# Where FoX's projection steps stand in a body of sixteen units: four together behind the first transposes, against two there and two ahead of the value products

## The chip, the cores and the metric

The kernel runs on one NeuronCore of a Trainium2 chip. The metric is the device time of one execution in microseconds (us). TensorE (PE) multiplies, and loads its stationary operand in a second instruction (PEld); VectorE (DVE), ScalarE (ACT) and GpSimd (POOL) work beside it, and SyncE (SP) issues DMAs. Each engine takes its own instructions in the order in which they are written and stops at a semaphore wait, with all that stands behind it.

## The reference

One layer of a hybrid decoder trunk over 1024 tokens of width 1024, in float32:

```
h = rms_norm(x); p = h @ w_in
x += concat[FoX attention | Mamba-2 SSD | GLA | HGRN2] @ w_out
x += cross_attention(rms_norm(x), rms_norm(mem))
x += conv_glu(rms_norm(x))
```

The change lies in FoX, the forgetting attention. It has 4 heads of width 64, and for each block of 128 queries it computes

```
logits = q @ k.T * scale + cum_log_f[query] - cum_log_f[key]   # keys up to the block's end
probs  = softmax(where(causal, logits, -1e30))
o      = probs @ v, then rms_norm over each head
```

## The kernel before

**Stages.** The mixers are computed one after another: HGRN2, FoX, SSD, GLA; then the output projection, cross attention and the feed-forward part. The one combined projection `h @ w_in` is not a stage of its own. It is cut into column groups of 128 ("items"), each item into two halves of 512 tokens, each half into 8 steps. A step (`fill`, line 1278) is three matmuls of 128x512, which take the float32 product as high times high, low times high and high times low part (lines 100 to 102). Steps of the next mixer are spread between the instructions of the present one, so that PE has work while ACT and DVE do softmax and evictions. Tables say how many steps stand at each place: `spread` (line 144) turns a list of counts into ranges of steps, and `_FX` (line 169) is the list for FoX. The first six counts are for FoX's preparation (`FOX_PRE`), the others come in pairs, one pair for each of the 16 units of the body: `FOX_A[u]` and `FOX_B[u]`.

**The body of FoX.** A unit u is a pair of heads and a block of 128 queries, i = u mod 8; its keys are i+1 blocks of 128. In this text the pieces of PE's work in a unit are called as follows:

- T0, T1 (line 1460): transposes of the probabilities of the two heads, key blocks 0 to 3 and, where i is 4 or more, 4 to 7. Each head's transposes wait for that head's exponential (`expd`), and for the eviction of the group two before in the same PSUM bank (`p_ev`).
- A and B: the steps `FOX_A[u]` and `FOX_B[u]`, two each before.
- S0, S1 (line 1450): the scores of unit u+2, keys 0 to 511 and, where they exist, the rest. A score piece goes to one of three banks in turn and waits until DVE has read the piece three before (`sc_read`).
- X (line 1441): small extra products, in units 1, 2, 3, 4, 9, 10, 11 (two) and 13.
- O (lines 1470 and 1476): the row sums' inverses spread over a bank, and the products of the probabilities with the values.

Their order on PE is T0, A, T1, S0, X, B, S1, O; in unit 0 A stands ahead of T0.

**The other engines in a unit.** ACT takes, in this order: the evictions of T0 and T1 (line 709), the eviction of X (line 692 or 687; for a norm lines 574 and 576), in every other unit the eviction of a projection half (`copy_out`, line 518), the exponentials of unit u+1 for both heads (line 699, each with an accumulator read that completes it), and in every fourth unit the high part of the next weights (line 505). DVE takes the inverse of the sums (1058), the normalisation of unit u-1 (1063, 1065), the logits of unit u+2 from the score banks (1039 and 1045), their maxima (1054), and at times the low part of the weights (852).

The choice of halves that ACT and DVE handle in a unit goes by the first step of `FOX_A[u]` and the last of `FOX_B[u]` (`begun`, line 161).

Of the kernel before, what the change touches and what calls it, by code (L numbers as in the profile page):

```python
# [21 lines left out]
KT = D // P  # L22
# [111 lines left out]
H0, F0, S0, G0 = 1, 9, 15, 21  # L134
# [9 lines left out]
def spread(first, last, counts):  # L144

    out, m = [], first
    for c in counts:
        out.append((m, m + c))
        m += c
    assert m == last  # L150
    return out
# [4 lines left out]
def in_two(spans):  # L156

    return spans[0::2], spans[1::2]
# [6 lines left out]

_HG = spread(2 * F0 * KT, 2 * S0 * KT, [16] * 4 + [2, 2] * NT)
HG_PREP, (HG_A, HG_B) = _HG[:4], in_two(_HG[4:])
_FX = spread(2 * S0 * KT, 2 * G0 * KT, [6, 6, 5, 5, 5, 5] + [2, 2] * 16)
FOX_PRE, (FOX_A, FOX_B) = _FX[:6], in_two(_FX[6:])
_SD = spread(2 * G0 * KT, 2 * N_ITEMS * KT, [12] * 4 + [5, 5] * 4 + [4, 4] + [0, 0] * 3)  # L170
SSD_CONV, (SSD_A, SSD_B) = _SD[:4], in_two(_SD[4:])
# [2333 lines left out]
```

How the kernel before makes its waits and increments, by code:

```python
            def link(ins):  # L257
                count[0] += 1
                ins.then_inc(E(s), 1)
                eng.wait_ge(E(s), count[0])
# [67 lines left out]
        @block.sync  # L328
        def _(sp):
            w = a["w_in"][0]
            narrow = ((0, OFF_FF, 4), (DT_ROW, OFF_DT, 4), (GA_ROW, OFF_GA, 16))
            def x_tile(i):
                sp.dma_start(MX[:, i, :], x[i * P:(i + 1) * P, :]).then_inc(x_loaded[i], 16)
            sp.dma_start(LNX, a["ln_mix"][0].partition_broadcast(P)).then_inc(E("ln_loaded"), 16)
            for i in range(3):
                x_tile(i)
            sp.wait_ge(E("zeroed"), 1)
            with nc.allow_non_contiguous_dma(reason="narrow column groups and parameter columns"):
                for row, off, n in narrow:
                    sp.dma_start(WR[:, 0, :, row:row + n], w[:, off:off + n].rearrange("(k p) c -> p k c", p=P))\
# [19 lines left out]
                                a["ssd_d"][0, h:h + 1].rearrange("(p o) -> p o", o=1).to_broadcast([64, 1])))  # L361
                for dst, src in par:
                    sp.dma_start(dst, src).then_inc(E("params"), 16)
                assert len(par) == N_PAR
            for n in range(RAW, N_ITEMS):
                sp.wait_ge(E("g_lo"), n - RAW + 1)
                if n == G0 + 3:
                    sp.wait_ge(E("av_ev"), len(PAIRS))
# [11 lines left out]
            for j in range(KV_ITEMS):  # L380
                if j == KV_ITEMS // 2:
                    sp.wait_ge(E("gl_e1"), 1)
                    sp.wait_ge(E("gl_e2"), 1)
```

## Time and profile before

| | |
|---|---|
| median of 3 runs | 1709.78 us (1709.38 to 1710.87) |
| the profiled execution | 1708.04 us, of which its span 1706.3 us |
| PE busy | 1641.3 us, 96% of the span |
| DVE, ACT, POOL busy | 794.6, 662.8, 74.3 us |
| TensorE's granted clock, mean | 0.989 |

The span runs from the first to the last instruction that the profile shows; 1.7 us of the execution lie around it. PE is the engine that is nearly always busy, and the chain of work that ended last runs over it. The FoX body lies from 294.5 us, where unit 0's A starts, to 408.7 us, where unit 15's O ends.

### The profile page before, as it was taken

To read this page: it belongs to the slowest core of one execution; us is meant where nothing else is said; L and a number is where in the kernel's file an instruction comes from. 1 tells how busy PE (TensorE), PEld (TensorE's weight loads), DVE (VectorE), ACT (ScalarE), POOL (GpSimd) and SP (SyncE) were. 2 spreads that over 40 slices of the span, in tenths; PEclk is the share of its full clock that TensorE was granted. 3 is DMA by queue.
4 is the path that set the end of the run, shared out by engine and by line. 5 is a ranking of instruction groups with operands and counts; after the bars stand their busy time and mean duration, and the time that the engine had idled before them with its cause. 6 is when DMAs were issued, how large, how long until landed. Compare 5 with 4: busy or idle time off the path is not lost.

```text
span 1706.3 us, 20672 instructions
## 1 busy us (share of the span) xinstructions
PE 1641.3 (96%) x8070; PEld 1318.6 (77%) x8070; DVE 794.6 (47%) x1315; ACT 662.8 (39%) x1194; POOL 74.3 (4%) x144
## 2 busy tenths in 40 slices
PE   6999999999998989999999999999999999999997
PEld 5888666667775567888888888888888888888886
DVE  5316534436667464533453255555433455555332
ACT  5225127456333463443432143444323334443221
POOL 2000210110102200000000000000000000000000
PEclk9999899999999999999999999999999999999999
DMA  5121000000112244000111133333232433332322
GB/s 151 50 51 38 26 13 25 21 18 30 58 38 87 69 160 155 4 22 1 38 56 38 37 99 99 93 93 93 74 99 89 128 98 118 94 98 93 99 96 96
DMA packets 166921, 121.31 MB, mean 71 GB/s; under 512 B 23448, under 2 KB 140456, under 8 KB 166824
## 3 DMA queue, kind: packets, MB, share of 16 engines
q1 hardware_dynamic: 165496, 115.53, 22.2%
q10 hardware_dynamic: 1328, 4.46, 0.7%
q8 instruction: 65, 1.06, 0.3%
q14 instruction: 32, 0.26, 0.0%
HBM read 115.77 MB, written 4.19 MB: 70 GB/s over the span
## 4 chain that ended last, share of the span: by engine, by line
PE 62%; DVE 1%; ACT 0%; issue 0%; DVEq 0%; ACTq 0%
PE tail_b L100 19%; PE tail_b L101 19%; PE tail_b L102 19%; PE tail_b L2345 2%; PE tail_b L2320 1%; PE tail_b L2309 0%; PE tail_b L2332 0%; PE tail_b L2256 0%; DVE tail_wl L2020 0%; PE tail_b L2380 0%; PE tail_b L2464 0%; DVE tail_xs L2055 0%; ACT tail_xs L1855 0%; DVE XR L2183 0%; PE tail_b L2393 0%
## 5 line engine op out<-in xcount | busy, mean ns | idle before, releaser
L2176 DVE TENSOR_TENSOR ff_wl<-ff_wr,ff_wh 128x512 fp32r<-128x512 f32 (+1 forms) x176 | 168.5, 958 | 329.9 <-ACT ff_wh L1963 329.9
L1963 ACT ACTIVATE ff_wh<-ff_wr 128x512 fp32r<-128x512 f32 (+1 forms) x176 | 148.7, 846 | 377.9 <-PE tail_b L102 377.8
L100 PE MATMUL tail_b<-HH,ff_wh 128*128 128x512 f32 x704 | 273.9, 389 | 0.0
L101 PE MATMUL tail_b<-HL,ff_wh 128*128 128x512 f32 x704 | 273.9, 389 | 0.0
L102 PE MATMUL tail_b<-HH,ff_wl 128*128 128x512 f32 x704 | 273.9, 389 | 0.0
L100 PE MATMUL mix_gb<-HH,mix_wh 128*128 128x512 f32 x432 | 182.5, 422 | 5.4 <-DVE mix_wl L852 5.3
L101 PE MATMUL mix_gb<-HL,mix_wh 128*128 128x512 f32 x432 | 169.9, 393 | 0.0
L102 PE MATMUL mix_gb<-HH,mix_wl 128*128 128x512 f32 x432 | 169.8, 393 | 0.0
L100 PE MATMUL tail_b<-tail_wh,HH 128*128 128x512 f32 x384 | 154.2, 402 | 6.0 <-DVE tail_wl L2020 4.8
L100 PEld LDWEIGHTS tail_b<-HH,ff_wh 128*128 128x128 f32 x704 | 132.2, 188 | 27.7
L102 PEld LDWEIGHTS tail_b<-HH,ff_wl 128*128 128x128 f32 x704 | 132.2, 188 | 27.3
L101 PEld LDWEIGHTS tail_b<-HL,ff_wh 128*128 128x128 f32 x704 | 132.2, 188 | 27.3
L102 PE MATMUL tail_b<-tail_wh,HL 128*128 128x512 f32 x384 | 150.7, 393 | 0.0
L101 PE MATMUL tail_b<-tail_wl,HH 128*128 128x512 f32 x384 | 150.6, 392 | 0.0
L100 PEld LDWEIGHTS mix_gb<-HH,mix_wh 128*128 128x128 f32 x432 | 82.3, 190 | 29.2 <-issue 7.0
L100 PE MATMUL tail_b<-ff_wh,ff_aha 128*128 128x512 f32 x256 | 100.2, 392 | 0.0
L101 PE MATMUL tail_b<-ff_wl,ff_aha 128*128 128x512 f32 x256 | 99.7, 389 | 0.0
L101 PEld LDWEIGHTS mix_gb<-HL,mix_wh 128*128 128x128 f32 x432 | 82.3, 191 | 18.4 <-issue 3.6
L102 PEld LDWEIGHTS mix_gb<-HH,mix_wl 128*128 128x128 f32 x432 | 82.0, 190 | 18.0
L100 PEld LDWEIGHTS tail_b<-tail_wh,HH 128*128 128x128 f32 x384 | 72.8, 190 | 21.1 <-DVE tail_wl L2020 5.2
L852 DVE TENSOR_TENSOR mix_wl<-mix_wr,mix_wh 128x1024 fp32r<-128x1024 f32 x43 | 53.0, 1232 | 76.4 <-ACT mix_wh L505 75.4
L102 PEld LDWEIGHTS tail_b<-tail_wh,HL 128*128 128x128 f32 x384 | 72.7, 189 | 15.7
(347 smaller groups left out, 2444.0 us busy)
## 6 DMA issues: line engine op xcount, KB each, us to landing
ff_wr<-in_ffn_w_up SPq DMA_DIRECT2D x88, 512.0 KB, 3.6
ff_wr<-in_ffn_w_down SPq DMA_DIRECT2D x88, 256.0 KB, 2.7
mix_wr<-in_w_in SPq DMA_DIRECT2D x26, 512.0 KB, 3.4
mix_wr<-in_xa_wkv SPq DMA_DIRECT2D x16, 512.0 KB, 3.6
XR<-in_x SPq DMA_DIRECT2D x8, 512.0 KB, 6.3
XR<-in_x ACTq DMA_DIRECT2D x1, 4096.0 KB, 18.8
tail_wr<-in_xa_wq SPq DMA_DIRECT2D x16, 256.0 KB, 4.0
tail_wr<-in_xa_wo SPq DMA_DIRECT2D x16, 256.0 KB, 3.3
```

The lines of the kernel that those rows point to most:

```text
L100: pe.matmul(out, hi_w, hi_x, start=first, stop=False)
L101: pe.matmul(out, hi_w, lo_x, start=False, stop=False)
L102: return pe.matmul(out, lo_w, hi_x, start=False, stop=last)
L852: dve.tensor_tensor(WL[:, n % PART, :, :], WR[:, n % RAW, :, :], WH[:, n % PART, :, :], ALU.subtract)\
L1963: act.activation(part(FWH[m % FPART], m), part(FWR[m % FRAW], m), ACT.Copy).then_inc(w_hi, 1)
L2176: dve.tensor_tensor(part(FWL[m % FPART], m), part(FWR[m % FRAW], m), part(FWH[m % FPART], m), ALU.subtract)\
L2320: mm = pe.matmul(bank[3 + g][:, hh * N_MEM:(hh + 1) * N_MEM], QT[:, 2 * h + kk, :], ktr(2 * h + kk), start=(kk == 0), stop=(kk == 1))
L2345: mm = pe.matmul(bank3[6 + g][:, j, :], vv(m, d), PT[:, m, d // 2, :], start=(m == 0), stop=(m == 1))
```

## The change

```diff
-_FX = spread(2 * S0 * KT, 2 * G0 * KT, [6, 6, 5, 5, 5, 5] + [2, 2] * 16)
+_FX = spread(2 * S0 * KT, 2 * G0 * KT, [6, 6, 5, 5, 5, 5] + [4, 0] * 16)
```

`FOX_A[u]` now has four steps and `FOX_B[u]` none, in each of the 16 units; the steps are the same ones in the same order. DVE, ACT, POOL and SP hold the same instructions in the same order as before. PE holds the same instructions in another order.

On PE in unit 1, from the scores (L1450) over the extra product (L1441) and the value products (L1470, L1476) to unit 2's transposes (L1460). L100 to L102 are the three matmuls of a projection step. Before:

```order
L1450 MATMUL mix_m<-XR 128x512 x2
L1441 MATMUL mix_m<-slots,ident 128x512
L100 MATMUL mix_gb<-HH,mix_wh 128x512
L101 MATMUL mix_gb<-HL,mix_wh 128x512
L102 MATMUL mix_gb<-HH,mix_wl 128x512
L100 MATMUL mix_gb<-HH,mix_wh 128x512
L101 MATMUL mix_gb<-HL,mix_wh 128x512
L102 MATMUL mix_gb<-HH,mix_wl 128x512
L1470 MATMUL mix_m<-ident,mix_rin 64x128 x2
L1476 MATMUL mix_m<-mix_scratch,slots 64x128 x4
L1460 MATMUL mix_m<-ident,slots 128x128 x6
```

After the change, the same stretch and the last step ahead of it:

```order
L100 MATMUL mix_gb<-HH,mix_wh 128x512
L101 MATMUL mix_gb<-HL,mix_wh 128x512
L102 MATMUL mix_gb<-HH,mix_wl 128x512
L1450 MATMUL mix_m<-XR 128x512 x2
L1441 MATMUL mix_m<-slots,ident 128x512
L1470 MATMUL mix_m<-ident,mix_rin 64x128 x2
L1476 MATMUL mix_m<-mix_scratch,slots 64x128 x4
L1460 MATMUL mix_m<-ident,slots 128x128 x6
```

The six matmuls between the extra product and the value products went to the place ahead of the scores.

On PE in unit 5, with bank numbers, from the scores of keys 0 to 511 (S0) over those of the other keys (S1) to the value products. Before:

```order
L1450 MATMUL mix_m2<-XR 128x512
L1450 MATMUL mix_m0<-XR 128x512
L100 MATMUL mix_gb0<-HH,mix_wh 128x512
L101 MATMUL mix_gb0<-HL,mix_wh 128x512
L102 MATMUL mix_gb0<-HH,mix_wl 128x512
L100 MATMUL mix_gb0<-HH,mix_wh 128x512
L101 MATMUL mix_gb0<-HL,mix_wh 128x512
L102 MATMUL mix_gb0<-HH,mix_wl 128x512
L1450 MATMUL mix_m1<-XR 128x512
L1450 MATMUL mix_m2<-XR 128x512
L1470 MATMUL mix_m5<-ident,mix_rin 64x128 x2
```

After the change, from unit 5's second transposes on:

```order
L1460 MATMUL mix_m3<-ident,slots 128x128 x2
L1460 MATMUL mix_m4<-ident,slots 128x128 x2
L1450 MATMUL mix_m2<-XR 128x512
L1450 MATMUL mix_m0<-XR 128x512
L1450 MATMUL mix_m1<-XR 128x512
L1450 MATMUL mix_m2<-XR 128x512
L1470 MATMUL mix_m5<-ident,mix_rin 64x128 x2
```

The four score pieces stand side by side now, and the fourth goes to the same bank, m2, as the first.

## Rows read from the trace of the kernel before

**Rows 1.** Stretches: busy us (instructions) of PE, PEld, DVE, ACT, POOL; clock; DMA.

```profile
286.00:294.50 8.50, 5.75 (x19) 2.43 (x17) 5.65 (x10) 5.86 (x9) 1.58 (x4) 1.00 0.00 0
294.50:408.70 114.20, 114.20 (x795) 77.97 (x794) 48.51 (x212) 64.73 (x142) 15.52 (x29) 1.00 0.07 19
```

**Rows 2.** Waits of the weight loads, 294 to 409: total us, times, longest.

```profile
PEld mix_m L1460 <- ACT slots L699: 0.9, 5, 0.2
```

**Rows 3.** Timeline of PE, unit 1: start, us, line, count.

```profile
302.39 1.12 PE L1441 MATMUL mix_m<-slots,ident 128*128 128x512 f32 x2
...
303.59 0.40 PE L101 MATMUL mix_gb<-HL,mix_wh 128*128 128x512 f32 x1
...
304.82 0.44 PE L1470 MATMUL mix_m<-ident,mix_rin 128*64 128x128 f32 x4
...
305.63 0.88 PE L1460 MATMUL mix_m<-ident,slots 128*128 128x128 f32 x6
306.26 0.49 PE L100 MATMUL mix_gb<-HH,mix_wh 128*128 128x512 f32 x1
```

**Rows 4.** Timeline of ACT, unit 1: X's eviction, the exponentials of unit 2.

```profile
303.62 0.60 ACT L692 ACTIVATE XR<-mix_m 128x512 f32<-128x512 f32 x1 [3.11 <-PE mix_m L1441]
...
305.21 0.19 ACT L699 ACTIVATION_READ_ACCUMULATOR slots<-slots,mix_nm 128x1 f32 x1
```

**Rows 5.** Timeline of PE, unit 14 and the first transposes of unit 15.

```profile
397.90 0.82 PE L1460 MATMUL mix_m<-ident,slots 128*128 128x128 f32 x6
398.48 0.48 PE L100 MATMUL mix_gb<-HH,mix_wh 128*128 128x512 f32 x1
398.80 0.40 PE L101 MATMUL mix_gb<-HL,mix_wh 128*128 128x512 f32 x1
...
399.72 0.39 PE L102 MATMUL mix_gb<-HH,mix_wl 128*128 128x512 f32 x1
400.04 0.44 PE L1470 MATMUL mix_m<-ident,mix_rin 128*64 128x128 f32 x4
...
401.93 1.09 PE L1460 MATMUL mix_m<-ident,slots 128*128 128x128 f32 x8
402.78 0.48 PE L100 MATMUL mix_gb<-HH,mix_wh 128*128 128x512 f32 x1
```

**Rows 6.** Timeline of ACT, unit 14: T1's eviction, the exponentials of unit 15.

```profile
398.43 0.88 ACT L709 ACTIVATE mix_scratch<-mix_m 128x384 f32<-128x384 f32 x2 [0.36 <-PE mix_m L1460]
...
401.84 0.21 ACT L699 ACTIVATION_READ_ACCUMULATOR slots<-slots,mix_nm 128x1 f32 x1
```

**Rows 7.** Timeline of PE, the first transposes of unit 10 and what follows.

```profile
362.91 1.06 PE L1460 MATMUL mix_m<-ident,slots 128*128 128x128 f32 x6
363.73 0.48 PE L100 MATMUL mix_gb<-HH,mix_wh 128*128 128x512 f32 x1
```

**Rows 8.** Timeline of ACT, the second exponential of unit 10 completes.

```profile
363.19 0.19 ACT L699 ACTIVATION_READ_ACCUMULATOR slots<-slots,mix_nm 128x1 f32 x1
```

**Rows 9.** Timeline of PE, unit 5: S0, B, S1.

```profile
331.86 1.13 PE L1450 MATMUL mix_m<-XR 64*128 64x512 f32 x4
332.92 0.50 PE L100 MATMUL mix_gb<-HH,mix_wh 128*128 128x512 f32 x1
...
334.52 1.13 PE L1450 MATMUL mix_m<-XR 64*128 64x512 f32 x4
```

**Rows 10.** Timeline of DVE, unit 5: the read of S0's first bank.

```profile
333.13 0.69 DVE L1039 CUSTOM_DVE_ANT_0 slots<-mix_m,slots 128x512 f32<-128x512 f32 x1 [3.39 <-PE mix_m L1450]
```

**Rows 11.** Timeline of PE ahead of the body: the fourth score piece, then projection.

```profile
293.91 0.70 PE L1450 MATMUL mix_m<-XR 64*128 64x256 f32 x2 [0.85 <-DVE mix_nmx L1045]
294.53 0.50 PE L100 MATMUL mix_gb<-HH,mix_wh 128*128 128x512 f32 x1
```

**Rows 12.** Timeline of DVE: the read for which that piece waited completes.

```profile
293.77 0.08 DVE L1045 DVE_READ_ACCUMULATOR2_ANT mix_nmx<- 128x1 f32 x1
```

**Rows 13.** Waits of PE behind FoX, 408 to 1706: the longest by one writer of weights.

```profile
PE tail_b L100 <- DVE tail_wl L2020: 4.8, 1, 4.8
```

## The prediction

> **What bounds the kernel now.** I read the share of busy time first: PE at 96%, the others at half or less, and the chain of waits runs over PE. Then the busy time by stretches: in the FoX body PE is busy for all of 114.2 us, at the full clock of 2.4 GHz [rows 1]. PE is the bound there, so whatever the change does, it does through PE: by what PE itself saves where it changes from one kind of matmul to another, and by any wait that it did not have. The list of waits shows PE's margin is thin: its weight loads at the transposes waited for an exponential of ACT five times in the body, by 0.9 us in all [rows 2]. So I then laid the timeline of PE beside those of ACT and DVE, unit by unit. The reader is to see there how long before its use each exponential is ready.
>
> A difference below 0.2% (3.4 us) can't be told from none in a measurement of this kernel; that is my bound for "same".
>
> **What is moved, and its price on PE alone.** No instruction is added or removed; the DMA queues and the orders of ACT, DVE and POOL stay. Two steps, six matmuls, leave the place B in each of 16 units. Inside a run of projection matmuls one follows another by 0.23 us (four intervals in 0.92 us, [rows 5]), so behind A they take 6 x 0.23 = 1.38 us. In their old place they take more, because the change to and from other matmuls costs something: in unit 14 from 398.48 to 400.04, 1.56 us; between S0 and S1 in unit 5 1.60 us [rows 9]. Behind an X it is less: X takes 303.59 - 302.39 - 0.23 = 0.97 us, and X with B takes 304.82 - 302.39 = 2.43 us, so B has 1.46 us there [rows 3]. If no wait came in, the 16 units would save 7 x 0.08 (one X) + 0.1 (two X) + 8 x 0.2, or 2.3 us.
>
> **What stood behind B.** Between X (or T1, or S0) of unit u and T0 of unit u+1, PE now has only O, and S1 in some units. In that same stretch ACT evicts X or T1, in even units a projection half, and then makes the two exponentials of unit u+1, for which T0 waits, head by head. ACT's row of work is as long as before and starts at the same event of PE. B was its cover, and A, which is longer now, stands on the other side of T0. Behind the waiting T0 stand all of PE's other work and, through it, everything else.
>
> Let m be the margin before: the time by which the second head's exponential was ready ahead of the point where PE wanted it. If m is below what B took, PE waits for the difference b - m, and it has paid 1.38 elsewhere for the b that it lost here. So the unit becomes longer by b - m + 1.38 - b = 1.38 - m. If m is larger, it becomes shorter by b - 1.38.
>
> The margins come from pairs of rows. From a DVE read that is complete at 293.85 to the piece that waited for it at 293.91 there are 0.06 us [rows 11, 12], and I take the same from ACT. In unit 1, T0 of unit 2 starts at 305.63; its second head is wanted half of 0.63 us later, at 305.94 [rows 3]; the exponential is complete at 305.21 + 0.19 = 305.40 [rows 4]; m = 0.48. In unit 14, 401.93 + 0.42 = 402.35 against 401.84 + 0.21 + 0.06 = 402.11 [rows 5, 6]; m = 0.24. In unit 9, PE wanted it at 362.91 + 0.31 = 363.22 and had it at 363.19 + 0.19 + 0.06 = 363.44: no margin, and in fact six transposes took 0.82 us there against 0.63 in unit 1 [rows 3, 7, 8]. That is one of the five waits, and it shows that the mechanism is at work already. The other 13 units are read in the same way.
>
> In us, 1.38 - m by unit: 0: 0.06; 1: 0.90; 2: 0.84; 3: 0.13; 4: 0.41; 6: 0.53; 9: 1.38; 10: 0.86; 11: 0.55; 13: 0.41; 14: 1.14. Together 7.2. Units 7, 8 and 15 have small exponentials or none behind them (margins over 2.5 us); they save 0.2 each: -0.6.
>
> **A second wait, in units 5 and 12.** There is no X between S0 and S1 there. S1's second head goes to the bank of S0's first head (m2 in unit 5), and waits until DVE has read it. S0 starts at 331.86, DVE at 333.13 for 0.69 us; with 0.06 on top the bank is free 2.02 us after S0's start [rows 9, 10]. S0 itself takes 332.92 - 331.86 = 1.06 us, so S1's second head stands 0.96 us. The kernel shows such a wait once already, before the body, where the fourth score piece waited 0.85 us for DVE [rows 11]. A late head of 512 columns runs alone for two passes, as X does, 0.97 us to about 1.05; of 256 columns it took 0.62 [rows 11]. So S0, the wait and S1 end about 3.0 us after S0's start, against 2.66 + 1.06 = 3.72 before. B's place gives back 0.7 of 1.38: the unit becomes longer by 0.7 us. Unit 12 (384 columns) comes to the same. Together 1.4. These two units have margins over 2 us at the next T0, so nothing comes on top. In the units with X, the 1.06 + 0.97 = 2.03 us just cover the 2.02.
>
> **The sum.** 7.2 + 1.4 - 0.6 = 8.0 us on PE in the body. Behind it PE waits for ACT and DVE here and there, the longest for weights 4.8 us [rows 13], but these wait for PE's own earlier work or for loads that are issued when an earlier item is done, so all of it moves with FoX's end. I count 8.0 in full. From 1708.0 us of the profiled execution that makes 1716.0; the median of the runs shown lies 1.7 above it, so the forecast for a median is 1717.8 us.
>
> Bounds. Each term rests on a margin read to about 0.05 us, but on chains that were not run in this order. From below: if no wait appeared, -2.3 us. From above: if each of the 11 units had no margin at all, 11 x 1.38 = 15.2, with 1.4 and -0.6: 16. I take the value worked out from the pairs, as ACT is one queue whose order is fixed and whose durations I have.
>
> **The clock.** The projection matmuls now come in one block in each unit, with up to 6 us of small matmuls and some waiting between blocks (unit 13: S0, X, S1, O, T0 and 0.6 of wait). From 286.0 to 294.5 PE did only such small products and stood still for 2.75 us of it, and the granted clock was 1.00 [rows 1]. The Trainium skill ("TensorE: Matmul & The Clock Gate", section "Part 4: PE-mode transpose") says that transposes don't count as busy time for the clock gate; by that rule the longer stretches would speak against the change. The trace does not show a fall in that stretch, though only part of it was transposes.
>
> **Rivals.**
> PE doesn't starve: the exponentials come in time, because less stands in ACT's way than I think (T0's evictions are long done when T1 comes). For it: PE's busy share in the body was 100%, so margins were positive nearly everywhere. Against it: the pairs give margins under 1.4 us in 11 of 16 units, and B's 1.5 us must come out of them. It decides where the mean margin is above 1.5. Then only the changes of matmul kind count: 1708.0 - 2.3 = 1705.7 on the profiled execution, 1707.4 on the median: not slower. Chance 0.06. If besides the four score pieces ran closer together than 1.06 us a pair, one more us or two would go: faster by over 3.4; 0.02 of it.
> The waits come, but about half as large: PE that is late at one T0 gives DVE and ACT time at the next, and a part is given back. 1713.5. For it: a delayed PE is a margin for others. Against it: the margins are within a unit, from an event of PE to an event of PE. Chance 0.10.
> More waits: weights' high and low parts (ACT 505, DVE 852) and squares come later behind the exponentials and hold T0's evictions and DVE's logits. A further 1 us in the four units with weights: 1722 to 1725. Chance 0.07.
> The clock falls to 1.2 GHz for a part of each unit. Twelve matmuls of 0.23 us would take 2.8 us more; in 15 units 42 us: 1760. Chance 0.02.
>
> **How the numbers follow.** The forecast's own case has 0.75 (0.06 + 0.10 + 0.07 + 0.02 for the others), with a range of 1714.5 to 1721. To leave out no more than 0.2 in all I take 1712.0 to 1722.5. Slower by over 3.4 us: the forecast, the clock, the more waits, and half of the half-size case: 0.89. Same: the rest of that, and most of the first rival: 0.09. Faster: 0.02.
>
> **What would show it.** Right: PE's waits at line 1460 for ACT's line 699 grow from 0.9 us to about 9 us over some 11 units, most behind units 9, 14, 1, 2 and 10; PE waits at line 1450 for DVE's 1039 in units 5 and 12, about 1 us each; the body lasts 122.2 us instead of 114.2, and each later stage has its old length. The clock stays at 1.00 in the body. Wrong: no idle time at 1460 and a body of 112; or a later stage that takes the 8 us back; or waits named at 1476 or at the projection's own matmuls (for p_ev, av_ev or g_lo), which I have at nothing.

## The result and the profile after

The changed kernel took 1722.92 us in the median of 4 executions (1719.79 to 1724.21), the kernel before 1709.58 us (1705.15 to 1710.87). The ratio is 1.008, with a 95% interval of 1.0057 to 1.0103: slower by 13 us. The forecast was 1717.8 us, with a range to 1722.5. The direction was right, and the time lies 0.4 us above the range.

The profiled execution of the changed kernel has a span of 1722.5 us, against 1706.3: 16.2 us more. The busy time by stretches shows where. The columns are the stretch in us from the span's start, its length, busy us and instructions of PE, PEld, DVE, ACT and POOL, the granted clock, and the DMA share and rate. Kernel before, up to the body, the body, the next 160 us, the rest:

```profile
0.00:294.53 294.53, 269.40 (x1372) 210.21 (x1372) 123.02 (x172) 117.68 (x199) 30.75 (x74) 0.98 0.20 51
294.53:408.74 114.21, 114.21 (x795) 77.97 (x795) 48.48 (x212) 64.70 (x142) 15.49 (x29) 1.00 0.07 19
408.74:568.74 160.00, 142.14 (x731) 109.11 (x729) 107.19 (x181) 62.81 (x95) 21.80 (x34) 0.96 0.18 60
568.74:1706.30 1137.56, 1115.54 (x5175) 921.29 (x5175) 515.87 (x752) 417.64 (x760) 6.26 (x8) 0.99 0.26 83
```

The changed kernel:

```profile
0.00:300.80 300.80, 275.50 (x1372) 213.95 (x1372) 123.96 (x172) 117.76 (x199) 29.61 (x74) 0.97 0.20 50
300.80:422.85 122.05, 116.85 (x795) 79.21 (x795) 47.94 (x212) 64.53 (x142) 15.48 (x29) 1.00 0.07 18
422.85:582.85 160.00, 142.20 (x725) 109.42 (x724) 106.83 (x180) 61.15 (x92) 21.36 (x34) 0.95 0.18 60
582.85:1722.50 1139.65, 1117.30 (x5183) 922.69 (x5181) 515.86 (x752) 418.93 (x763) 6.63 (x10) 0.99 0.26 83
```

The body takes 122.05 us in place of 114.21: 7.84 more, where the prediction had 8.0. PE was busy in all of it before; now it has nothing to run (it stands dry) for 122.05 - 116.85 = 5.2 us, and its weight loads wait longer than that. The other 8.3 us lie outside the body, in code where no instruction differs: 6.3 ahead of it and 2.1 behind it.

The waits of the weight loads in the body after the change, in us, times and longest; line 1460 had 0.9 us before [rows 2]:

```profile
PEld mix_m L1460 <- ACT slots L699: 9.3, 19, 1.5
...
PEld mix_m L1450 <- DVE mix_nmx L1039: 6.3, 8, 0.9
```

The second line counts all time in which the weights for a score piece could have been loaded earlier. Most of it lies beside running matmuls: the units that pay for it, 5 and 12, become longer by 1.5 us together (the table below).

Unit 1 on PE, to be laid beside [rows 3]: X, O and the first transposes of unit 2, and the projection behind them.

```profile
310.13 1.13 PE L1441 MATMUL mix_m<-slots,ident 128*128 128x512 f32 x2
311.19 0.44 PE L1470 MATMUL mix_m<-ident,mix_rin 128*64 128x128 f32 x4
...
312.60 1.15 PE L1460 MATMUL mix_m<-ident,slots 128*128 128x128 f32 x6 [0.54 <-ACT slots L699]
313.50 0.48 PE L100 MATMUL mix_gb<-HH,mix_wh 128*128 128x512 f32 x1
```

And ACT there, beside [rows 4]:

```profile
311.35 0.60 ACT L692 ACTIVATE XR<-mix_m 128x512 f32<-128x512 f32 x1 [3.99 <-PE mix_m L1441]
...
312.95 0.19 ACT L699 ACTIVATION_READ_ACCUMULATOR slots<-slots,mix_nm 128x1 f32 x1
```

ACT's row is as long as it was: from X's start to the second exponential 313.14 - 310.13 = 3.01 us, before 305.40 - 302.39 = 3.01 us. PE's way shrank from 3.24 us (302.39 to 305.63) by the 1.37 us of B, and PE stands until the exponentials are there.

Unit 14, beside [rows 5], shows both heads waiting, 0.35 and 0.47 us dry:

```profile
412.33 0.82 PE L1460 MATMUL mix_m<-ident,slots 128*128 128x128 f32 x6
413.07 0.44 PE L1470 MATMUL mix_m<-ident,mix_rin 128*64 128x128 f32 x4
...
415.39 0.66 PE L1460 MATMUL mix_m<-ident,slots 128*128 128x128 f32 x4 [0.35 <-ACT slots L699]
416.51 0.66 PE L1460 MATMUL mix_m<-ident,slots 128*128 128x128 f32 x4 [0.47 <-ACT slots L699]
416.93 0.48 PE L100 MATMUL mix_gb<-HH,mix_wh 128*128 128x512 f32 x1
```

In unit 5 the four score pieces, S0 and S1, stand together (beside [rows 9]). From the first to the value products they take 3.08 us; two pairs without a wait take 2 x 1.06.

```profile
341.75 3.15 PE L1450 MATMUL mix_m<-XR 64*128 64x512 f32 x8
344.83 0.44 PE L1470 MATMUL mix_m<-ident,mix_rin 128*64 128x128 f32 x4
```

DVE's read of the bank for which the fourth piece waits, beside [rows 10]: it ends at 343.71, 1.96 us after S0's start.

```profile
343.02 0.69 DVE L1039 CUSTOM_DVE_ANT_0 slots<-mix_m,slots 128x512 f32<-128x512 f32 x1 [4.42 <-PE mix_m L1450]
```

Unit by unit, from the start of one A to that of the next, in us of difference to before:

| unit | 0 | 1 | 2 | 3 | 4 | 5 | 6 | 7 | 8 | 9 | 10 | 11 | 12 | 13 | 14 | 15 |
|---|---|---|---|---|---|---|---|---|---|---|---|---|---|---|---|---|
| forecast | 0.06 | 0.90 | 0.84 | 0.13 | 0.41 | 0.7 | 0.53 | -0.2 | -0.2 | 1.38 | 0.86 | 0.55 | 0.7 | 0.41 | 1.14 | -0.2 |
| measured | 0.07 | 0.90 | 0.82 | 0.08 | 0.37 | 0.75 | 0.45 | -0.22 | -0.23 | 1.34 | 0.84 | 0.52 | 0.74 | 0.38 | 1.07 | -0.04 |

So the question was where the rest comes from.

### The profile page after: what moved, and what is told of

Read it like the earlier page. It is cut to its first block, busy times and chain, and to the rows that moved or that the text cites. A ratio compares the mean times of both kernels' runs of the same rounds, so it can differ in the third digit from the quotient of the medians.

```text
span 1722.5 us, 20672 instructions
## 1 busy us (share of the span) xinstructions
PE 1651.8 (96%) x8070; PEld 1325.3 (77%) x8070; DVE 794.6 (46%) x1315; ACT 662.4 (38%) x1194; POOL 73.1 (4%) x144
## 4 chain that ended last, share of the span: by engine, by line
PE 61%; DVE 1%; ACT 0%; issue 0%; DVEq 0%; ACTq 0%
PE tail_b L100 19%; PE tail_b L102 19%; PE tail_b L101 19%; PE tail_b L2345 2%; PE tail_b L2320 1%; PE tail_b L2309 0%; PE tail_b L2332 0%; PE tail_b L2256 0%; DVE tail_wl L2020 0%; PE tail_b L2380 0%; PE tail_b L2464 0%; DVE tail_xs L2055 0%; ACT tail_xs L1855 0%; DVE XR L2183 0%; PE tail_b L2393 0%
## 5 line engine op out<-in xcount | busy, mean ns | idle before, releaser
L100 PE MATMUL tail_b<-HH,ff_wh 128*128 128x512 f32 x704 | 274.1, 389 | 0.0
L102 PE MATMUL tail_b<-HH,ff_wl 128*128 128x512 f32 x704 | 274.1, 389 | 0.0
L100 PE MATMUL mix_gb<-HH,mix_wh 128*128 128x512 f32 x432 | 180.8, 419 | 5.4 <-DVE mix_wl L852 5.3
L102 PE MATMUL mix_gb<-HH,mix_wl 128*128 128x512 f32 x432 | 171.8, 398 | 0.0
L100 PE MATMUL tail_b<-tail_wh,HH 128*128 128x512 f32 x384 | 154.5, 402 | 6.0 <-DVE tail_wl L2020 4.8
L102 PEld LDWEIGHTS tail_b<-HH,ff_wl 128*128 128x128 f32 x704 | 132.2, 188 | 27.3
L100 PEld LDWEIGHTS tail_b<-HH,ff_wh 128*128 128x128 f32 x704 | 132.2, 188 | 27.2
L102 PE MATMUL tail_b<-tail_wh,HL 128*128 128x512 f32 x384 | 151.0, 393 | 0.0
L100 PEld LDWEIGHTS mix_gb<-HH,mix_wh 128*128 128x128 f32 x432 | 83.4, 193 | 25.3 <-DVE mix_wl L852 6.2
L100 PE MATMUL tail_b<-ff_wh,ff_aha 128*128 128x512 f32 x256 | 100.3, 392 | 0.0
L102 PEld LDWEIGHTS mix_gb<-HH,mix_wl 128*128 128x128 f32 x432 | 83.3, 193 | 18.3
L100 PEld LDWEIGHTS tail_b<-tail_wh,HH 128*128 128x128 f32 x384 | 72.9, 190 | 21.0 <-DVE tail_wl L2020 5.2
L102 PEld LDWEIGHTS tail_b<-tail_wh,HL 128*128 128x128 f32 x384 | 72.8, 190 | 15.7
```

The lines of the kernel that those rows point to most:

```text
L100: pe.matmul(out, hi_w, hi_x, start=first, stop=False)
L102: return pe.matmul(out, lo_w, hi_x, start=False, stop=last)
```

## The experiments

Two quantities are read from each profile beside the time: the body (from the first A to the projection behind unit 15's O) and what lies ahead of and behind it. A fall of the clock is a stretch of some microseconds in which the granted clock of TensorE is 1.2 GHz in place of 2.4. Of each execution there are also the span and the mean granted clock; their product is about what the span would be at the full clock, and wanders a little less.

**The two kernels again (e1, e2, e10, e11).** No edit.

> The changed kernel once more, nothing edited. Its first profile had a body of 122.05 us (before 114.21) but also 6.3 us more ahead of the body and 2.1 us more behind it, where no instruction differs. Theory 'chance of the clock': the body repeats to 0.3 us, at about 122.0, and what lies outside it wanders by some us from execution to execution with the granted clock; outside the body it comes to anything from 1590 to 1601 us, and the ratio of times settles near 1.005 (+8 to +9 us). Rival 'the change costs clock outside the body': outside stays near 1600 us, 8 us above the kernel before, and the ratio stays near 1.008.

> The kernel before once more, nothing edited. Body 114.2 us by both. 'Chance of the clock': outside the body it wanders from 1590 to 1601 us, as the changed kernel does, and can come as high as the changed kernel's. Rival 'the change costs clock': outside stays at 1592 us to 2 us. Time against itself: ratio 1.000.

> The changed kernel a third time. If the falls behind the body belong to the program, they come out as in its two profiles, 1299.65 us, while ahead of the body it wanders (300.8 and 297.5 so far). If they are chance, another value between 1294 and 1301. Body 122.05. Mean time above before's by 11 us if the excess over the body's 7.84 is lasting, by 8 to 9 if it was chance.

> The kernel before a third time. Falls belong to the program: 1297.5 us behind the body again. Chance: another value. Body 114.2.

| profile | ahead | body | behind | span |
|---|---|---|---|---|
| before | 294.53 | 114.21 | 1297.6 | 1706.3 |
| before again | 298.87 | 114.25 | 1297.5 | 1710.6 |
| before, third | 297.43 | 114.21 | 1298.3 | 1709.9 |
| changed | 300.80 | 122.05 | 1299.6 | 1722.5 |
| changed again | 297.49 | 122.05 | 1299.7 | 1719.2 |
| changed, third | 294.62 | 122.04 | 1299.6 | 1716.3 |

The bodies repeat to 0.04 us. Ahead of the body both kernels wander over the same 6 us (294.5 to 298.9, and 294.6 to 300.8), so the 6.3 us of the first pair of profiles were chance. Behind it the changed kernel is slower by 1.4 to 2.2 us every time. Each kernel has the falls of its clock behind the body at its own places, the same ones in its three profiles. The 1298.3 us of before's third profile, in place of the 1297.5 expected, lie behind PE's last matmul: that matmul ends 1287.1 to 1287.3 us behind the body in all three, and 1289.2 to 1289.4 us in the changed kernel's three, 2.1 us later in the mean. Neither theory was right as it stood: the part ahead is chance, the part behind is lasting.

The times agree. The changed kernel's ratio was 1.0065 (1.0046 to 1.0083) and then 1.0057 (1.0042 to 1.0072); before against itself 0.9994 (0.998 to 1.0008). Over all 16 executions of the changed kernel the mean span is 1719.5 us; over the 88 executions of before that were timed with the experiments it is 1708.7, 10.8 us apart. Span times clock gives 1694.0 and 1685.7, 8.3 us apart, close to the body's 7.84. The rest is lower clock. The medians of the same two groups are 1721.6 and 1710.6 us, 11.0 apart. In the first comparison before's four executions happened to lie 1.0 below that and the changed kernel's 1.3 above, which makes its 13.3. A single execution of before took anything from 1704.8 to 1717.6 us.

**The early exponentials (e3).**

```diff
-                for g in range(i // 4 + 1):
+                probs_out(u, 0)
+                if u + 1 < len(PAIRS):
+                    fox_exp(u + 1)
+                for g in range(1, i // 4 + 1):
                     probs_out(u, g)
 ...
-                if u + 1 < len(PAIRS):
-                    fox_exp(u + 1)
```

> The changed kernel, and ACT makes the exponentials of unit u+1 right behind the eviction of T0, ahead of the evictions of T1, X and the projection half. Theory 'ACT's row behind X and T1 is what T0 waits for': the waits at 1460 for 699 go from 9 us (and 4.6 us in which PE had run dry) to under 1 us, the waits at 1450 for DVE in units 5 and 12 stay at about 1 us each, and the body is 113.4 us (114.2 before, less 2.3 for the changes of matmul kind and old waits, and 1.4 for the two bank waits). Rival 'the exponential is late because its own input (maxima) is late, or PE has no other work': body stays at 120 or more.

The body was 114.30 us, and the weight loads at the transposes waited for the exponentials once, for 0.2 us, in place of 9.3 us. The unit with the largest loss, 9, went from +1.34 to -0.23. Units 5 and 12 kept theirs (+0.72, +0.74), as the other theory of the prediction has it. ACT's row behind X and T1 is what T0 waited for: shown. The 0.9 us by which 113.4 was too low is the term of the changes of matmul kind. ACT in unit 1 here, the exponentials ahead of X's eviction:

```profile
304.60 0.63 ACT L699 ACTIVATE slots<-slots,mix_nm 128x384 f32<-128x384 f32 x1
305.11 0.21 ACT L699 ACTIVATION_READ_ACCUMULATOR slots<-slots,mix_nm 128x1 f32 x1
307.79 0.60 ACT L692 ACTIVATE XR<-mix_m 128x512 f32<-128x512 f32 x1 [2.47 <-PE mix_m L1442]
```

And PE there (the lines are one further down): X to O to T0 without a gap.

```profile
306.57 1.12 PE L1442 MATMUL mix_m<-slots,ident 128*128 128x512 f32 x2
307.62 0.44 PE L1471 MATMUL mix_m<-ident,mix_rin 128*64 128x128 f32 x4
...
308.43 0.88 PE L1461 MATMUL mix_m<-ident,slots 128*128 128x128 f32 x6
```

The time was 1710.98 us, ratio 1.0004 (0.9989 to 1.0018).

**Four steps behind T0 in five units only (e4).** The table is `(4, 0) if u in (1, 2, 9, 10, 14) else (2, 2)`.

> Four steps behind T0 only in the five units with the smallest margins (1, 2, 9, 10, 14); two and two in the others. Theory 'a unit pays 1.38 us less its margin': 0.90 + 0.84 + 1.38 + 0.86 + 1.14 = 5.1 us more than before, body 119.3 us. Rival 'every unit pays the same share' (5 of 16 of 7.84): 2.5 us, body 116.7 us.

The body was 119.12 us: 0.86, 0.80, 1.36, 0.84 and 1.08 in the five units and 0.03 or less in the others. The units don't help or hurt each other by more than 0.03 us, and they don't pay equal shares. The time's ratio was 1.0045 (1.0028 to 1.0061), 7.4 us in the medians for 4.9 in the body.

**The half's eviction behind the exponentials (e7).**

```diff
                 new = range(*begun((FOX_A[u][0], FOX_B[u][1])))
-                for m in new:
-                    copy_out(m)
                 if u + 1 < len(PAIRS):
                     fox_exp(u + 1)
+                for m in new:
+                    copy_out(m)
```

> The changed kernel, and ACT evicts the projection half behind the exponentials of unit u+1 instead of ahead of them, in even units. Theory 'T0 waits for ACT's row': one eviction (0.48 us) leaves the row in even units; units 0, 2, 4, 6, 10 and 14 get shorter by 0.28, 0.48, 0.39, 0.48, 0.48 and 0.48, the others stay; the body is 119.5 us. Rival 'the exponential's input or PE is late': body stays at 122.0.

The body was 119.48 us. Against the changed kernel units 0, 2, 4, 6, 10 and 14 came down by 0.31, 0.50, 0.38, 0.46, 0.48 and 0.50. The eviction takes 0.48 us of ACT's row (319.22 to 319.70 in unit 2 of the changed kernel; the profile shows it busy for 0.59, beside the exponential). Taken out, it comes back one to one on PE where PE had waited for at least as long; units 0 and 4 had waited for less. Its one timed execution, 1712.93 us, says little.

**Early exponentials, units 5 and 12 at two and two (e8).**

> The early exponentials with four steps behind T0, except in units 5 and 12, which have two and two again. Theory 'S1's second head waits for DVE's read of its bank, in units 5 and 12 alone': each gives back 0.73, the body is 112.8 us, 1.4 less than before. Rival 'the wait goes elsewhere': 113.5 or more. The time can't show 1.4 us for certain; by the body 0.1% faster than before, if the clock's falls behind it don't change.

The body was 112.85 us, and units 5 and 12 were back at -0.02 and 0.02. The bank that DVE still reads is the whole loss of these two units: shown. The time was 1707.9 us, ratio 0.9981 (0.997 to 0.9992), the lowest of all versions tried; 1.36 us of the difference is the body; span times clock is 1.8 us below before's.

**Early exponentials on the old table (e12).** The edit of e3 on the kernel before.

> The kernel before (two and two steps) with the early exponentials alone. Theory 'the table costs only through ACT's row and the two bank waits': the old waits go (0.2 us behind unit 9 and little else), the body is 114.0 us; so with early exponentials four steps behind T0 are 1.1 us better than two and two (112.85 measured with units 5 and 12 left out), where they were 7.8 us worse. Rival 'the early exponentials themselves gave the gain': body 113.0 or less. The time: within 0.1% of before, apart from the clock falls behind the body.

The body was 114.40 us, not 114.0. Unit 9 gave back its old wait (-0.18), but units 4 and 13 got longer by 0.16 and 0.24. The profile names a new wait of 0.2 us, X's for T1's eviction, now behind the exponentials on ACT:

```profile
PE mix_m L1442 <- ACT mix_scratch L709: 0.2, 1, 0.2
```

So the early exponentials alone bring nothing here, and with them four and none is better than two and two by 1.5 us of body in units other than 5 and 12. The time was 1.0021 of before (1.0007 to 1.0036) with 0.2 us in the body: spans are 3.5 us longer in the mean, span times clock 0.3. An interval that excludes 1 can come from the clock alone at this size, and that holds for e8's as well.

**A delay of the same length in the old order (e5, e6, e9).** Extra matmuls into unused columns of the output bank, in unit 8 of the kernel before:

```diff
                 pe.wait_ge(E("rin"), u + 1)
+                if u == 8:
+                    for _ in range(66):
+                        pe.matmul(M[5][:, 2 * P:4 * P], HH[:, 0, 0:P], HH[:, 0, 0:2 * P], start=True, stop=True,
+                                  skip_group_check=True)
```

> The kernel before, with 42 extra matmuls (128x256, into unused columns of a bank) ahead of unit 8's value products: an estimate of 8 us of pure delay in the body and nothing else. Two profiles of the kernel before took 1297.5 us behind the body and two of the changed kernel 1299.7 us, each pair with the same clock falls at the same places. Theory 'FoX's later end moves where the clock falls': a body longer by about 8 us for whatever reason gives the falls of the changed kernel, 1299.7 behind, and the time is up by the pad and 2 to 3 us more. Rival 'the new order itself costs clock': behind stays at 1297.5, and the time is up by the pad alone.

> The same with 21 matmuls, an estimate of 4 us. 'Later end moves the falls': behind the body neither 1297.5 nor 1299.7 need come out; some other value between 1294 (seen with the early exponentials) and 1301 (seen with five units changed). 'The order costs clock': 1297.5.

> The kernel before with 66 extra matmuls in unit 8, at 0.12 us each (42 of them took 5.02 us, not the 8 of the estimate): a body longer by 7.9 us, 122.1 in all, as in the changed kernel, with the order of before. Theory 'FoX's later end moves the clock falls': behind the body 1299.7 and the falls of the changed kernel; the mean time is above before by 10 to 12 us. Rival 'the order costs clock': 1297.5 behind and +8 to +9 us. Third, 'falls behind the body differ from program to program with no rule that the end's place sets': any other value between 1294 and 1301.

42 matmuls took 5.02 us, not 8, so e5 could not decide what it was made for: its body was 119.25 us, behind it 1297.2, its ratio 1.0032 (1.0019 to 1.0046). With 21, the body was 116.66 and behind it 1298.7 us, another value than 1297.5. With 66 the body was 122.12 us. Its stretches, to be read beside the changed kernel's above:

```profile
300.46:422.58 122.12, 122.12 (x861) 86.07 (x860) 48.48 (x212) 64.67 (x142) 15.49 (x29) 1.00 0.07 18
422.58:582.58 160.00, 142.19 (x725) 109.37 (x724) 106.82 (x180) 61.26 (x92) 21.45 (x34) 0.95 0.19 60
582.58:1722.10 1139.52, 1117.13 (x5182) 922.92 (x5180) 516.13 (x752) 418.66 (x763) 6.53 (x9) 0.99 0.27 83
```

Behind the body it took 1299.6 us, as the changed kernel does, with its clock falls in the same stretches of 10 us, and its ratio was 1.007 (1.0053 to 1.0087); its mean span is 12.4 us above before's, a little over the 10 to 12 expected. So the new order costs no clock of its own at this length of body: a body that ends 7.9 us later by extra matmuls has the same falls behind it as one that ends 7.8 us later by waits. One of them, 68 us behind the body's end, in the SSD stage. In the 10 us that begin 60 us behind the body's end PE is busy for 7.36 us in both kernels (the counts differ, as not every matmul is recorded). The granted clock there is 1.00 before:

```profile
468.74:478.74 10.00, 7.36 (x49) 5.93 (x49) 5.19 (x14) 2.55 (x4) 0.61 (x2) 1.00 0.16 54
```

and 0.83 in the changed kernel:

```profile
482.85:492.85 10.00, 7.36 (x37) 5.61 (x36) 5.10 (x13) 2.55 (x4) 0.61 (x2) 0.83 0.17 54
```

Kernel before, PE there:

```profile
477.00 0.39 PE L102 MATMUL mix_gb<-HH,mix_wl 128*128 128x512 f32 x1
477.23 0.49 PE L1516 MATMUL mix_m<-ident,slots 128*128 128x128 f32 x3
```

The same matmul in the changed kernel, and the one ahead of it:

```profile
491.61 0.63 PE L101 MATMUL mix_gb<-HL,mix_wh 128*128 128x512 f32 x1
492.04 0.63 PE L102 MATMUL mix_gb<-HH,mix_wl 128*128 128x512 f32 x1
```

One matmul follows the other by 0.43 us there in place of 0.23: the clock is at 1.2 GHz, not 2.4.

The falls account for what lies behind the body in every profile. The time at 1.2 GHz is read from the granted clock, without the low stretch behind PE's last matmul. Matmuls follow one another there at about half the rate (0.43 us in place of 0.23 above), so where PE is the bound half of that time is lost:

| profile | body | behind | of it at 1.2 GHz | behind less half of that |
|---|---|---|---|---|
| before, three times | 114.2 | 1297.5 to 1298.3 | 20.5 | 1287.2 to 1288.0 |
| changed, three times | 122.0 to 122.1 | 1299.6 to 1299.7 | 23.9 | 1287.7 |
| e3 | 114.3 | 1294.2 | 13.7 | 1287.4 |
| e4 | 119.1 | 1300.8 | 27.3 | 1287.2 |
| e5 | 119.3 | 1297.2 | 20.5 | 1286.9 |
| e6 | 116.7 | 1298.7 | 23.9 | 1286.8 |
| e7 | 119.5 | 1295.7 | 17.1 | 1287.1 |
| e8 | 112.9 | 1297.0 | 20.5 | 1286.8 |
| e9 | 122.1 | 1299.6 | 23.9 | 1287.6 |
| e12 | 114.4 | 1297.5 | 20.5 | 1287.3 |

The times behind differ by 6.6 us and the last column by 1.2. The changed kernel is at 1.2 GHz for 3.4 us more than before: 1.7 of its 2.1 us.

How many falls there are follows no simple rule of the body's end. Bodies of 119.12, 119.25 and 119.48 us (e4, e5, e7) had 1300.8, 1297.2 and 1295.7 behind them, and 114.30 (e3) had 1294.2 where 114.21 had 1297.6. What decides this stays open.

## Why the prediction was wrong, step by step

- *PE bounds the body, and the change acts through PE.* Right. In the body DVE, ACT and POOL are busy for as long as before, to 0.6 us.
- *A unit with margin m becomes longer by 1.38 - m.* Right in all 11 units, to 0.08 us. Three experiments took the rule apart: without ACT's row the loss is gone (e3), with 0.48 us less in the row it falls by 0.48 (e7), and units pay one by one (e4).
- *The second wait, in units 5 and 12, 0.7 each.* Right: 0.75 and 0.74, and given back in full by two and two (e8).
- *Changes of matmul kind save 0.08 behind an X and 0.2 elsewhere, 2.3 us in all if no wait came in.* Too large, and hidden by the waits. X followed by O takes 1.06 us (310.13 to 311.19), not the 0.97 that I took from X followed by a projection matmul, so B cost 1.37 there and not 1.46. Without waits units 1, 2, 3, 4, 10, 11 and 13 are within 0.05 us of before (e3), units 14 and 15 save 0.03 and 0.04, and only 0, 6, 7 and 8 save 0.20 to 0.24 (the 0.23 of unit 9 is mostly its old wait). In the forecast this touched unit 15 alone (-0.2 against -0.04).
- *"I count 8.0 in full", and "each later stage has its old length".* The first half held, 7.84 us. The second is the step that failed: it put the stretch behind the body at nothing, and that stretch became longer by 2.1 us. PE's waits there hardly changed (29.4 us in all before, 29.7 after, the longest 4.8 in both), but the granted clock did: 23.9 us at 1.2 GHz in place of 20.5, which is 1.7 us. My clock rival asked only whether the clock falls inside the body (it stayed at 1.00); I had no term for falls elsewhere. A delay of the same length without the new order brings the same falls (e9), so they come with the shift of the body's end.
- *The median lies 1.7 us above the profiled execution.* Also too small: over 88 executions before's median is 1710.6, so 2.6 above that one. The range had no room for executions that wander by 6 us either way. The changed kernel's median over all 16 is 1721.6: 3.8 above the forecast, of which 0.9 is this level, some 2 the stretch behind the body, and 1 is not accounted for by a term; the part ahead of the body wanders by more than that. The further 1.3 us of the first four executions, 1722.92, are chance. That the result lies above the range at all rests on them, as 1721.6 lies inside it; the missing 2.1 us do not.
- The rivals: PE did not stay fed, the waits were not half-size, and no weights came late (the body shows no wait for `p_ev`, `av_ev` or `g_lo` that was not there before). In the body the clock stayed at 1.00 though 6.6 us passed between two blocks of projection matmuls in unit 13. By the rule of the Trainium skill ("TensorE: Matmul & The Clock Gate", "Part 4: PE-mode transpose"), that transposes don't count as busy in the way that other matmuls do, a fall was possible there; the trace shows none, though transposes are only part of that stretch.

## What to carry to other kernels

When filler work is moved on the bounding engine, list for each wait behind its old place how early its releaser was ready. The unit gets longer by the filler's length less that margin. The loss can be won back by moving the releaser forward on its own engine (e3), which brought nothing where the filler still covered it (e12). Before a moved block is priced, look which engine queue runs beside the gap that it leaves, and whether a bank is rewritten by two neighbours that it kept apart. On a kernel whose executions wander by 6 us, read a 1 to 8 us change from the stretch itself, which repeated to 0.04 us, and keep a few us in the range for the clock elsewhere.

## What the runs showed of the hardware that was not expected

- The places where the clock falls behind the body are a property of the program: the same in three profiles of the changed kernel, although what lies ahead of the body took 294.6, 297.5 and 300.8 us in them, and the same in three of before (294.5, 297.4 and 298.9 us). Ahead of the body they wander between executions of one program.
- A program of another order with the same length of body (122.12 against 122.05 us) had the same falls, 1299.6 us behind; bodies that differ by 0.1 us with another order on ACT and PE (114.30 and 114.21) had 1294.2 and 1297.6.
- The same stretch of the SSD stage, with PE busy for 7.36 of 10 us in both kernels, got a clock of 1.00 in one and 0.83 in the other.
- A 128x256 matmul of 32-bit high parts in an unbroken run of 42 or 66 took 0.12 us each (5.02 and 7.91 us in all), although each loads its weights anew and the weight loads shown for such matmuls last 0.19 us.
